# Group C of a two-layer encoder: outputs kept undivided by the softmax sum, two mixes moved a step, last transposes ahead of a score item

## The reference

```python
logits = einsum('bqhid,bshid->bhiqs', qb, k) * scale      # i = 0, 1: two maps a head
p = softmax(logits + bias, axis=-1)
a = p[:, :, 0] - lam * p[:, :, 1]
o = einsum('bhqs,bshe->bqhe', a, v)
o = rmsnorm(o, subln) * (1.0 - lam_init)                  # over the 64 channels of a head
```

## Time and profile before

| | us |
|---|---|
| median of 3 runs | 2949.53 |
| lowest, highest | 2949.03, 2953.87 |
| the profiled execution, its own time | 2959.07 |
| its span, first to last instruction | 2957.3 |
| group C of layer 0 (steps with C items) | about 335 to 478 of the span |

### The profile page before, as it was taken

How to read it: one execution, slowest core, us unless ns; L and a number is a source line. 1 busy time by engine, 2 the same in 40 slices (tenths; PEclk the granted TensorE clock), 3 DMA queues, 4 the chain that set the end, 5 groups by cost and what they waited for, 6 DMA issues and landing times.

```text
span 2957.3 us, 36854 instructions
## 1 busy us (share of the span) xinstructions
PE 2864.6 (97%) x13552; PEld 2275.1 (77%) x13552; DVE 1991.4 (67%) x2316; ACT 1315.0 (44%) x1844; POOL 460.7 (16%) x243
## 2 busy tenths in 40 slices
PE   7999889999999999999999998899999999999998
PEld 6777646888888888888877785478788888888887
DVE  3987888982465565556678888889716555565555
ACT  4327888993322222222333288889724122222223
POOL 2111332233300000000131123322241000000002
PEclk9999999999999999999999999999999999999999
DMA  5455332431221111111135533244212111112102
GB/s 199 161 163 128 86 83 61 103 104 58 57 59 56 43 43 56 43 43 43 42 134 203 172 92 72 65 88 109 97 46 69 43 58 43 43 43 66 47 29 57
DMA packets 236532, 236.67 MB, mean 80 GB/s; under 512 B 59520, under 2 KB 199680, under 8 KB 236416
## 3 DMA queue, kind: packets, MB, share of 16 engines
q1 hardware_dynamic: 236416, 235.13, 28.1%
HBM read 184.24 MB, written 50.86 MB: 79 GB/s over the span
## 4 chain that ended last, share of the span: by engine, by line
PE 82%; DVE 10%; issue 4%; ACT 3%; DMA 1%; SPq 0%; ACTq 0%; POOL 0%; DVEq 0%
PE ps L1837 31%; PE ps L1852 16%; PE ps L1574 11%; PE ps L1676 9%; PE ps L1551 5%; PE ps L1714 4%; PE ps L1715 3%; DVE ps L1270 2%; PE ps L1817 1%; PE ps L1710 1%; DVE r L1255 1%; PE ps L1605 1%; DVE r L1298 0%; DVE r L1292 0%; DVE ch L1222 0%
## 5 line engine op out<-in xcount | busy, mean ns | idle before, releaser
L1676 PE MATMUL ps<-stack 128*128 128x512 f32 (+1 forms) x1152 | 350.5, 423 | 45.5 <-ACT prob L942 17.9
L1468 DVE TENSOR_TENSOR xT<-ps,xT 128x512 f32<-128x512 f32 x352 | 241.5, 691 | 209.8 <-PE ps L1852 209.5
L1676 PEld LDWEIGHTS ps<-stack 128*128 128x128 f32 (+1 forms) x1152 | 209.7, 194 | 160.1 <-ACT prob L942 51.5
L1551 PEld LDWEIGHTS ps<-ident_r,prob_r 128*128 128x128 f32 x2048 | 233.2, 143 | 101.3 <-issue 23.9
L942 ACT ACTIVATE prob<-ps,nmx 128x1024 f32<-128x1024 f32 x256 | 285.2, 1114 | 20.9 <-PE ps L1551 10.7
L1433 DVE SCALAR_TENSOR_TENSOR cv<-u,vec,cv 128x1024 f32<-128x1024 f32 x176 | 225.8, 1283 | 89.0 <-ACT cv L1083 78.7
L1378 DVE TENSOR_TENSOR ptl<-ps,pth 128x512 fp32r<-128x512 f32 x384 | 256.5, 685 | 38.6 <-ACT pth L1004 34.8
L1095 ACT ACTIVATE ah<-cv 128x1024 fp32r<-128x1024 f32 x44 | 46.7, 1061 | 528.9 <-DVE cv L1446 528.9
L1837 PE MATMUL ps<-xgh,w0h 128*128 128x512 f32 x704 | 274.7, 390 | 0.0
L1837 PE MATMUL ps<-xgl,w0h 128*128 128x512 f32 x704 | 273.9, 389 | 0.0
L1837 PE MATMUL ps<-xgh,w0l 128*128 128x512 f32 x704 | 273.9, 389 | 0.0
(11 more groups left out here) (245 smaller groups left out, 5555.6 us busy)
## 6 DMA issues: line engine op xcount, KB each, us to landing
wraw<-in_w_up SPq DMA_DIRECT2D x88, 512.0 KB, 5.0
draw<-in_w_down SPq DMA_DIRECT2D x22, 1024.0 KB, 4.9
stack<-ka_d SPq DMA_DIRECT2D x64, 256.0 KB, 5.6
wraw<-in_w_in SPq DMA_DIRECT2D x30, 512.0 KB, 4.2
vst<-v_d SPq DMA_DIRECT2D x48, 256.0 KB, 3.8
x_d<-xT SPq DMA_DIRECT2D x2, 4096.0 KB, 17.6
wraw<-in_w_out SPq DMA_DIRECT2D x16, 512.0 KB, 5.2
stack<-qc_d SPq DMA_DIRECT2D x64, 128.0 KB, 3.5
```

Source lines behind the costliest of these rows:

```text
L1468: ins = dve.tensor_tensor(xs, ps[:, 4 + j % 4, :], xs, ALU.add)
L1551: return pe.transpose(dst.bitcast(F32R), src, ident_r[:, :])
L1676: ins = pe.matmul(score_banks(i)[:, kh, :], st[q][0:rows, c0:c0 + P], st[k][0:rows, kh * HALF:(kh + 1) * HALF], start=n == 0, stop=n == le ...
```

## The change

The sums of the first maps go into a buffer of their own, `csum`, which lives through all of group C. The outputs of C are no longer divided: `dinv`, its transposes, `nrm`, `osum`, `hi_mix` and `lo_mix` fall away for C, and ACT copies the value product from PSUM into `xg_plain` (the memory of `xgh`) at step 3 of the next unit. POOL works out eps 64 s0 s0 in unit 30 (`floor_c`, two instructions on 128x32), and one more matmul puts it under the sums of squares. `MIX_STEPS` puts mix 1 at step 3 and mix 2 at step 5. In step 7 of a C unit the transposes go ahead of the score item.

```diff
-MIX_STEPS = {1: 0, 4: 1, 6: 2, 7: 3}
+MIX_STEPS = {1: 0, 3: 1, 5: 2, 7: 3}
...
+                def floor_c():
+
+                    pool.wait_ge(c_out, (l + 1) * 2 * NC)
+                    settle(pool)
+                    pool.tensor_scalar(cfloor[:, :], csum[:, :], cst[:, C_EPS + 1:C_EPS + 2], None, ALU.mult).then_inc(c_floor_half, 1)
+                    pool.wait_ge(c_floor_half, l + 1)
+                    pool.tensor_tensor(cfloor[:, :], cfloor[:, :], csum[:, :], ALU.mult).then_inc(c_floor, 1)
...
                 def copy_part(x):
 
                     if x["group"] == "C":
+                        rows = slice(HD * x["par"], HD * x["par"] + HD)
+                        act.wait_ge(av_done, l * (8 * NU) + x["u"] * 8 + 8 + AV_CREDIT)
+                        act.activation(mix_at(xg_plain, x), ps[rows, 6 + x["half"], :], ACT.Copy).then_inc(c_out, 1)
                         return
...
                     if x["group"] == "C":
-                        dve.wait_ge(av_done, l * (8 * NU) + x["u"] * 8 + 8 + AV_CREDIT)
-                        dve.wait_ge(norm_copied, l * NU + x["u"] + 1 + N_CREDIT)
-                        dve.wait_ge(mix_lo, l * NU + x["u"] + MIX_CREDIT)
-                        dve.tensor_tensor(osum[rows, :], ps[rows, 6 + x["half"], :], nrm[rows, :], ALU.mult).then_inc(o_ready, 1)
                         return
...
+                    if c == 0:
+                        pe.wait_ge(c_floor, l + 1)
+                        pe.matmul(ps[:, 2, 0:4 * TT], ident, cfloor[:, :], start=True, stop=False)
...
-                        if after and s in EARLY_STEP_OF[after["group"]]:
-                            score_item(after, EARLY_STEP_OF[after["group"]][s])
+                        early = EARLY_STEP_OF[after["group"]].get(s) if after else None
+                        behind = x["group"] == "C" and s == 7
+                        if early is not None and not behind:
+                            score_item(after, early)
...
                         ins.then_inc(trans_done, 1)
+                        if early is not None and behind:
+                            score_item(after, early)
```

More of the change, by code:

```diff
@@ L430, in build, with sum_column @@
         crep, crep_r = ([a[:, 2 * c:2 * c + 2, :].rearrange("p m n -> p (m n)") for c in range(2)] for a in (ptf, ptf_r))
+        def sum_column(x, q):
+            return 2 * (x["h"] // 2 * TT + x["half"] * 4 + q) + x["h"] % 2
         def second_map(q):
@@ L727, in mix_maps @@
                     pool.wait_ge(mixed_first, n)
-                def sum_c():
-                    for c in range(2):
-                        pool.tensor_tensor(prob1a[:, c, :], xgh[:, 6 + c, :].bitcast(F32), xgl[:, 6 + c, :].bitcast(F32), ALU.add).then_inc(c_summed, 1)
+                def floor_c():
[4 more added lines that the diff above has]
+                    pool.tensor_tensor(cfloor[:, :], cfloor[:, :], csum[:, :], ALU.mult).then_inc(c_floor, 1)
                 def pool_unit(x, prev, nx, after):
                     if x["k"] == NU - 2:
-                        sum_c()
+                        floor_c()
                     second = nx and nx["group"] == "C"
@@ L1013, in act_unit @@
                         if x["k"] == NU - 1 and s < 2:
[L1014 to L1015 removed]
+                            act.wait_ge(c_out, (l + 1) * 2 * NC)
+                            act.activation(prob1b[:, s, :], xg_plain[:, 6 + s, :], ACT.Square).then_inc(c_squared, 1)
                         if x["k"] == NU - 1 and s == 5:
                             act.wait_ge(c_stat, l * 2 + 2)
[L1018 removed]
+                            act.activation(croot[:, :], ps[:, 2, 0:4 * TT], ACT.Sqrt, scale=1.0 / HD).then_inc(c_root, 1)
                         if x["k"] == NU - 1 and s >= 6:
@@ L1334, in mix_maps @@
                     dve.wait_ge(exp_done, l * NS + x["item0"] + 2 * i + 2 + EXP_CREDIT)
-                    a, c = slice(2 * i, 2 * i + 1), slice(2 * i + 1, 2 * i + 2)
+                    c = slice(2 * i + 1, 2 * i + 2)
                     step(dve.reciprocal(rinv[:, b, c], rsum[:, b, c]))
-                    ratio = dve.tensor_scalar(rinv[:, b, c], rsum[:, b, a], small[:, 4:5], rinv[:, b, c], ALU.mult, ALU.mult)
+                    n = sum_column(x, i)
+                    ratio = dve.tensor_scalar(rinv[:, b, c], csum[:, n:n + 1], small[:, 4:5], rinv[:, b, c], ALU.mult, ALU.mult)
                     if i in POOL_MIXES:
@@ L1389, in scale_c @@
                     dve.wait_ge(c_spread, l * 2 + c + 1)
-                    dve.scalar_tensor_tensor(two(prob1b[:, c, :]), two(prob1a[:, c, :]), small[:, 5:6], ps[:, 2 * c:2 * c + 2, :],
+                    dve.scalar_tensor_tensor(two(prob1b[:, c, :]), two(xg_plain[:, 6 + c, :]), small[:, 5:6], ps[:, 2 * c:2 * c + 2, :],
                                              ALU.mult, ALU.mult).then_inc(c_normed, 1)
@@ L1721, in sum_squares_c @@
                         o = 2 * (c * TT + m)
-                        ins = pe.matmul(ps[:, 2, o:o + 2], prob1b[:, c, m * P:(m + 1) * P], blk[:, 0:P:HD], start=True, stop=True)
+                        ins = pe.matmul(ps[:, 2, o:o + 2], prob1b[:, c, m * P:(m + 1) * P], blk[:, 0:P:HD], start=False, stop=c == 1 and m == TT - 1)
                     ins.then_inc(c_stat, 1)
```

64 lines of the change are left out of this document (42 added, 22 removed).

## The result

The changed kernel took 2969.72 us (median of 4 runs, 2968.23 to 2972.59), the kernel before, run beside it, 2950.95. The ratio is 1.0059, with a 95% interval of 1.0046 to 1.0072: slower by 0.6%, where 2967 had been forecast. The profiled executions have spans of 2957.3 and 2970.6 us, 13.3 apart, against 18.8 between the medians: the profiled run of before, at 2959.07, lies 8 us over its median.

What follows compares the result with a forecast made beforehand. C units were taken as bound by DVE waiting in turns with PE and ACT, then by DVE's unbroken work, not by one full engine. Median 2949.5 + 14.6 for two layers + 3 for PE's clock = 2967 us, range 2946 to 2986.

Steps and rivals of the forecast that it cites:

- a ring of 7.00: In unit 9, where DVE waits for PE: minimum, exponential, score matmuls, next minimum; two turns, 3.49 and 3.51 us, together 7.00.
- a stretch of DVE: In unit 9, from the minimum of step 3 to that of step 7, DVE never waits: 10.36 us before the change.
- D_1: Start of the DVE minimum of step 1 in a unit; the number after D is the step.
- 0.61 less a unit: DVE's dropped multiplication into `osum` in C units: a gain of 0.61 us each, if nothing takes its place.
- The hold: In C units, mix 1, issued 0.4 us after POOL's add began, is held until that add ends; unit 18.5 us.
- the faster rival: Mix 1 in C units is not held; the unit takes 16.75 us and the time is 2938; chance 14%.
- Units 9 to 14: Units 9, 10, 13, 14 lose 1.15 us each, units 11 and 12 0.75 each, all reaching 18.5.
- Units 7 and 8: First C units: mix 1 held by POOL, partly absorbed by DVE's gaps and waits; losses 1.2 and 0.35 us.
- The sum: All unit losses and gains added, without PE's clock: 7.3 us slower a layer, 14.6 for two layers.
- the tail: POOL's two adds of unit 30 go, one small matmul comes, under 0.3 us a layer; taken as 0.
- The clock term: PE's clock falls in four of 14 C units while PE idles: 3 us, bounds 0 and 20.
- The rival of 1.5 us a unit: Mix 1 held and PE's clock falling in most C units, 1.5 us each: 2984; chance 10%.

## Why the prediction was right

- *What bounds the unit.* The split into a ring of 7.00 and a stretch of DVE held: D_1 to D_3 stayed at 3.50, and where mix 1 was free the unit was 7.00 + 9.75 = 16.75 (run at 16.74 to 16.77 in units 9 to 13 of three kernels). That number had been worked out, not seen. "0.61 less a unit" for `osum` holds only there: in the old order DVE waits for scores instead, and the unit stays at 17.36.
- *The hold.* Mix 1's issue (1.64 after D_3 forecast, 1.66 measured), its end after POOL (1.09, measured 1.08) and D_3 to D_4 (4.62, measured 4.62) came from rows of another instruction, a plain TENSOR_TENSOR, and one partial overlap. The order's margin of 0.4 us, on which the faster rival hung, was there: 0.41. "3.1 instead of 1.3" was 3.04. With the rule of the Trainium skill (page "SBUF — State Buffer", section "Who interferes with whom"), that whoever issues first keeps the pair of ports for the whole instruction and the other is blocked, the traces agree: mix 1, issued second, ended 1.08 or 1.09 after the add in 16 of 16 units, and after half the add as well, with 1.94 us.
- *Units 9 to 14.* Forecast 18.5 for both halves; measured 18.51, 18.67, 18.50 and 18.80 for units 9 to 12, the excess over 18.50 being the clock's.
- *Units 7 and 8.* 1.55 together was forecast. D_1 of unit 9 moved from 377.34 to 379.34, and D_1 of unit 7 by 0.14: 1.86. Up to D_7 of unit 8 it is 1.42, and the rest is a thing that I hadn't listed. ACT's rounding of the last B output now stands in front of an exponential; before, it began at 373.52, ahead of D_7 (373.85). From the timeline of the changed kernel, D_7 of unit 8 and what follows:

```profile
375.41 1.23 DVE L1291 CUSTOM_DVE_ANT_0 ps<-ps,dtab 128x1024 f32<-128x1024 f32 x1
376.51 0.63 ACT L1013 ACTIVATE xgh<-osum 64x512 fp32r<-64x512 f32 x1
...
377.16 1.11 ACT L956 ACTIVATE prob1a<-ps,nmx 128x1024 f32<-128x1024 f32 x1
```

 The exponential starts 1.75 after D_7 instead of 1.32, and D_1 follows 3.93 after D_7 instead of 3.49: 0.4.
- *The sum.* 7.3 a layer was forecast, and from the first minimum of C to the output projection 6.98 and 6.69 were lost. Two misses cancel in it. At the first minimum of group A (477.60 to 486.30, and 1932.03 to 1947.19) 8.17 and 8.61 were lost, where the terms up to there, without the clock, add up to 7.65; behind it 1.2 and 1.9 came back, where 0.3 had been put for unit 15 and nothing for the tail. What gave it back no run shows. The span grows by 13.3, against 14.6 and 3 for the clock.
- *The clock term was too large.* It was put at 3, from a fall at unit 8 that stretched the ring. The clock did fall in nearly every C unit, as the gap in front of the score item let expect (the gap forecast at 2.4 us is 2.41). But here the slow matmuls mostly stand beside DVE's contiguous stretch, which hides them. They cost 1.0 over units 9 to 13 of both layers, so some 1.4 over the fourteen (an estimate from those ten). The rival of 1.5 us a unit did not happen in this kernel. In the kernel before with the mixes moved, where the gap is 3.25 us and ACT has the division's two instructions ahead of an exponential of the ring, something of its size did, and so it did in one unit with the mixes back (18.92).
- *From the median.* The forecast started from 2949.5. The medians lie 18.8 apart (13.6 to 21.2 by the interval of the ratio) and the spans 13.3, and the sum of terms, without the clock's, is 14.6. Some 5 us between medians and traces are not accounted for. The medians of the kernel before moved between 2951.7 and 2954.2 in later comparisons on other chips. So the sign and the hold are shown, but the closeness of 2967 to 2969.7 is partly luck: the terms in the traces are worth less than forecast, and the medians differ by more.
- *The rest.* Transposes first: 0 forecast, 0 measured in the two orders with mix 1 at step 3, perhaps a loss of 0.2% in the old one. ACT's copy at step 3: hidden, as forecast (0.58 us at 383.94, the exponential behind it not waited for by VectorE, which is held). Undivided outputs in the old order: not forecast alone. In DVE's order before, the first row is the minimum of step 3 (380.85), not of step 2 as written above it.

## What to carry to other kernels

Before moving a VectorE instruction with two SBUF inputs, look at what GpSimd has under way at its new place: if that one was issued first and reads SBUF, the VectorE instruction ended 1.08 us after it here (of the 1.28 that it takes alone), however short the overlap. The cure can lie on the other engine: here GpSimd's input computed one step sooner turned a loss of 0.6% into a gain of 0.5%, with the same work. And an edit that takes work off an engine can be worth 0.2% in one order and 0.5 to 0.9% in another, so it pays to measure order and work apart.

## What the runs showed of the hardware that I had not expected

- The end of the held instruction is exact: POOL's end plus 1.08 or 1.09 us, with 0.26, 0.86 or 1.96 us of overlap, so even 0.26 us of it is visible as 1.34 in place of 1.28.
- The same fall of TensorE's clock to its lower level (1.2 GHz) costs 0.0 to 0.3 us where its matmuls lie beside VectorE's stretch (units of 18.50 to 18.80), and 1.58 us in the one unit where they lay in the ring (18.92 against 17.34). In the kernel before with the mixes moved it seems to cost 1 to 2 us, most of it after the clock is back, by way of what ScalarE has to do ahead of an exponential.
- Matmuls added into TensorE's idle time kept its clock at 1.00 at no cost that the time shows when they needed no late result (2969.92 against 2969.72 us), and cost 15 us in all when their bank hung on one.
